# Differential attention on one Trainium2 core: steps of two query tiles in place of one

## What is computed

```
def attend_block(q_blk):
    s = jnp.einsum('mbhqd,mbhkd->mbhqk', q_blk, k).astype(jnp.float32) * scale
    p = jax.nn.softmax(s, axis=-1)
    a = p[0] - lam * p[1]
    return jnp.einsum('bhqk,bhkv->bhqv', a.astype(v.dtype), v)
...
o = rmsnorm(o, sub_gain) * (1.0 - lambda_init)
return o @ w_o
```

## Time and profile before

| | us |
|---|---|
| device time, median of 3 runs | 983.8 |
| lowest, highest | 982.41, 983.94 |
| span of the profiled execution, first to last instruction | 980.4 |
| attention in it, from the first scores to the MLP's first product | 77.8 to 281.3 |
| busy in the span: TensorE | 967.6 |
| VectorE | 853.5 |
| ScalarE | 457.9 |
| GpSimd | 377.8 |

### The profile page before, as it was taken

How to read it: one execution, slowest core, us unless ns; L and a number is a source line. 1 busy time by engine, 2 the same in 40 slices (tenths; PEclk the granted TensorE clock), 3 DMA queues, 4 the chain that set the end, 5 groups by cost and what they waited for, 6 DMA issues and landing times.

```text
span 980.4 us, 12869 instructions
## 1 busy us (share of the span) xinstructions
PE 967.6 (99%) x4684; PEld 796.9 (81%) x4684; DVE 853.5 (87%) x1157; ACT 457.9 (47%) x703; POOL 377.8 (39%) x333
## 2 busy tenths in 40 slices
PE   9999999989999999999999999999999999999998
PEld 7887877767887878888888888988888888888887
DVE  6696999999777999999989888779898988989883
ACT  6445654666556253552534534475345253452520
POOL 6841453335463828467534000551340413405000
PEclk9999999999999999999999999999999999999999
DMA  7333220200251432423334250304342332422202
GB/s 264 87 107 102 72 65 1 65 22 22 66 171 44 135 123 87 129 87 101 114 87 128 65 172 23 129 1 129 87 129 87 108 107 87 129 86 86 87 1 86
DMA packets 50966, 90.12 MB, mean 92 GB/s; under 512 B 8268, under 2 KB 9560, under 8 KB 50904
## 3 DMA queue, kind: packets, MB, share of 16 engines
q1 hardware_dynamic: 45456, 89.14, 29.0%
q10 hardware_dynamic: 5448, 0.17, 0.3%
HBM read 87.20 MB, written 2.10 MB: 91 GB/s over the span
## 4 chain that ended last, share of the span: by engine, by line
PE 63%; DVE 5%; POOL 2%; issue 1%; ACT 1%; POOLq 0%; DVEq 0%; ACTq 0%
PE bank L1711 32%; PE pair L1711 30%; POOL s_nsum L766 1%; DVE s_acc L1476 1%; DVE s_lbB_lo L1225 1%; DVE s_lt_lo L1225 1%; DVE s_w_lo L1198 1%; DVE s_acc L1545 0%; DVE s_s_raw L1461 0%; PE bank L2070 0%; DVE s_u_raw L1443 0%; PE pair L2058 0%; DVE s_hT_lo L1425 0%; POOL s_lt L792 0%; ACT s_hT_hi L1037 0%
## 5 line engine op out<-in xcount | busy, mean ns | idle before, releaser
L792 POOL TENSOR_TENSOR s_lt<-s_lbB,s_lbB 128x1024 f32<-128x1024 f32 x14 | 34.5, 2466 | 263.4 <-PE pair L1711 163.9
L1198 DVE TENSOR_TENSOR s_w_lo<-s_raw,s_w_hi 128x1024 fp32r<-128x1024 f32 x72 | 127.5, 1791 | 3.7 <-ACT s_w_hi L871 3.7
L1225 DVE TENSOR_TENSOR s_lbB_lo<-s_lbB,s_b_hi 128x1024 fp32r<-128x1024 f32 x64 | 119.0, 1883 | 0.0
L893 ACT ACTIVATE s_b_hi<-s_lbB 128x1024 fp32r<-128x1024 f32 x64 | 67.2, 1053 | 77.0 <-POOL s_lbB L792 32.9
L1711 PE MATMUL bank<-s_hT_hi,s_w_hi 128*128 128x512 f32 x256 | 100.2, 392 | 0.0
L1711 PE MATMUL pair<-s_hT_hi,s_w_hi 128*128 128x512 f32 x256 | 100.1, 391 | 0.0
L1711 PE MATMUL bank<-s_hT_hi,s_w_lo 128*128 128x512 f32 x256 | 99.6, 389 | 0.0
L1711 PE MATMUL bank<-s_hT_lo,s_w_hi 128*128 128x512 f32 x256 | 99.6, 389 | 0.0
L1711 PE MATMUL pair<-s_hT_hi,s_w_lo 128*128 128x512 f32 x256 | 99.6, 389 | 0.0
L1711 PE MATMUL pair<-s_hT_lo,s_w_hi 128*128 128x512 f32 x256 | 99.6, 389 | 0.0
L1057 ACT ACTIVATE s_u_raw<-s_u_raw 128x512 f32<-128x512 f32 x64 | 40.4, 632 | 111.6 <-DVE s_u_raw L1443 111.6
(11 more groups left out here) (268 smaller groups left out, 2699.3 us busy)
## 6 DMA issues: line engine op xcount, KB each, us to landing
s_raw<-in_mlp_w SPq DMA_DIRECT2D x64, 512.0 KB, 3.7
s_lbB<-in_mlp_w SPq DMA_DIRECT2D x64, 512.0 KB, 3.3
s_raw<-in_attn_w_qkv SPq DMA_DIRECT2D x24, 512.0 KB, 4.1
s_raw<-in_attn_w_o SPq DMA_DIRECT2D x8, 512.0 KB, 3.3
s_x_nat<-in_x SPq DMA_DIRECT2D x4, 512.0 KB, 6.4
out<-s_acc SPq DMA_DIRECT2D x7, 256.0 KB, 2.0
s_raw<-in_pool_w SPq DMA_DIRECT2D x4, 256.0 KB, 2.7
out<-s_acc SPq DMA_DIRECT2D x2, 128.0 KB, 1.8
```

The source lines that it names most:

```text
L792: g.tensor_tensor(w2_raw[n][:], w2_raw[one][:], w2_raw[two][:], ALU.subtract).then_inc(t_done, 1)
L893: a.activation(b_hi[home][:], w2_raw[n][:], ACT.Copy).then_inc(w2_hi_done, 1)
L1198: v.tensor_tensor(w_lo[slot][:, cols], raw[k][:], f32(w_hi[slot][:, cols]), ALU.subtract)\
L1225: v.tensor_tensor(w2_lo[n][:], w2_raw[n][:], f32(b_hi[home][:]), ALU.subtract).then_inc(w2_lo_done, 1)
```

## The change

A step `j` now handles a pair of query tiles, 2j and 2j+1, in 16 steps and a tail. The scores have four banks (both `pair` tensors, one per tile), the exponentials three buffers. The maxima of both maps of a tile are one reduction of 1024. Reciprocal and factor are computed once for a pair. The turned maps go to banks 4 and 5, which the sides use as well (q and k bank 4, o and the new turn back bank 5). `values(p)` takes V as weights and the turned maps of both tiles as moving operand, three matmuls of 256 columns per block of keys, so that o arrives transposed in bank 6. ScalarE copies it once per head (`keep_values`), TensorE turns it back (`turn_back`), ScalarE copies that (`keep_back`), and the statistics, the scaling and the turn of o follow as before. `o_keep` is gone. All fillers but the first use bank 7. The tables and the order in every engine's loop are written anew. The diff, cut to its core: lines of before that are replaced are left out where they stand in the listing above.

```
...
+    (((9, 0), (0, 1)), ((9, 1), (2,))),
+    (((10, 0), (0, 1)), ((10, 1), (2,))),
+    (((11, 0), (0, 1)), ((11, 1), (2, 3))),
+    (((12, 0), (0, 1)), ((12, 1), (2, 3))),
+    (((13, 0), (0, 1, 2)), ((13, 1), (3, 4))),
+    (((14, 0), (0, 1, 2)), ((14, 1), (3, 4))),
+    (((15, 0), (0, 1, 2)), ((15, 1), (3, 4, 5))),
+    (((16, 0), (0, 1, 2)), ((16, 1), (3, 4, 5))))
+X_SUMMED = (8, 8, 9, 10, 11, 12, 13, 14)
+X_ADDED = (11, 12, 13, 14, 15, 16, 18, 18)
+def filler_places():
+    at = {(u // 2, u % 2): divmod(max(u - 1, 0), 3) for u in range(2 * F_V)}
+    at |= {(f, u): (f - F_V + 5, u) for f in range(F_V, F_Y) for u in range(2)}
+        at |= {(f, u): place for u, (place, _) in enumerate(W_O_PARTS[f - F_Y])}
+FILL = filler_places()
+FILLED = {f: max(place for (g, _), place in FILL.items() if g == f) for f in range(F_END)}
+FILL_BANK = {f: 7 if f else 6 for f in range(F_END)}
+SPLIT = {4: (0, 0, 1, 1), 5: (2, 2, 3, 3), 6: (5, 5, 6, 6), 7: (10, 12, 13, 14), 8: (17, 17, 18, 18)}
...
+QK_SIDE = {j: (what, n) for j, what, n in SIDE if j >= 0 and what != "o"}
+O_SIDE = {j: (what, n) for j, what, n in SIDE if what == "o"}
...
         def turn_bank(what, n):
-            return bank[2 + n % 2] if what == "map" else bank[4]
+            if what == "map":
+                return bank[4 + n % 2]
+            return bank[5] if what == "o" else bank[4]
         def turn_scale(what):
...
+            def exps(n):
+                if n >= 3:
+                    act.wait_ge(turned, n - 2)
+                act.wait_ge(max_done, n + 1)
...
+                    a.activation(probs[n % 3][:, m, :], pair[n % 2][:, m, :], ACT.Exp,
+                                 bias=nmax[:, n % 4, m:m + 1],
+                                 accum_out=lsum[:, n, m:m + 1]).then_inc(exp_done, 1)
...
+            def keep_values(h):
+                act.wait_ge(pv_done, 2 * h + 2)
+                if h:
+                    act.wait_ge(back_turned, h)
+                a.activation(ov[:], bank[6][:], ACT.Copy).then_inc(ov_kept, 1)
+            def keep_back(h):
+                act.wait_ge(back_turned, h + 1)
+                if h:
+                    act.wait_ge(side_turned, SIDE_NO["o", h - 1] + 1)
+                a.activation(oc[:], bank[5][:], ACT.Copy).then_inc(back_kept, 1)
+            for j in range(END):
+                for f in range(F_END):
+                    if FILLED[f] == (j - 1, 2) or F_V <= f < F_Y and FILLED[f] == (j - 1, 1):
+                        filled(f)
+                if j < PAIRS:
+                    exps(2 * j)
+                for f in range(F_END):
+                    if FILLED[f] == (j, 0):
+                        filled(f)
+                if 1 <= j <= PAIRS:
+                    keep_turn("map", 2 * j - 2)
+                    keep_turn("map", 2 * j - 1)
+                if j < PAIRS:
+                    exps(2 * j + 1)
+                for f in range(F_END):
+                    if FILLED[f] == (j, 1) and not F_V <= f < F_Y:
+                        filled(f)
+                if j in QK_SIDE:
+                    keep_turn(*QK_SIDE[j])
+                if j in BACK:
+                    keep_back(BACK[j])
+                if j in KEPT:
+                    keep_values(KEPT[j])
+                if j in O_SIDE:
+                    keep_turn(*O_SIDE[j])
...
+            def maxima(n):
+                dve.wait_ge(scored, n + 1)
+                v.tensor_reduce(nmax[:, n % 4, :], pair[n % 2][:], AX.X, ALU.max, negate=True).then_inc(max_done, 1)
+            def mix_root(p):
+                dve.wait_ge(exp_done, 4 * p + 4)
+                v.reciprocal(rl1[:, p % 2, :], lsum[:, 2 * p:2 * p + 2, 1]).then_inc(mix_rooted, 1)
+            def mix_factor(p):
+                dve.wait_ge(mix_rooted, p + 1)
+                v.scalar_tensor_tensor(mixc[:, p % 2, :], lsum[:, 2 * p:2 * p + 2, 0], neg_lam[:, 0:1],
+                                       rl1[:, p % 2, :], ALU.mult, ALU.mult).then_inc(mix_known, 1)
+            def combine(n):
+                dve.wait_ge(mix_known, n // 2 + 1)
+                both = probs[n % 3]
+                v.scalar_tensor_tensor(both[:, 0, :], both[:, 1, :], mixc[:, n // 2 % 2, n % 2:n % 2 + 1], both[:, 0, :],
                                        ALU.mult, ALU.add).then_inc(a_done, 1)
+            def o_stats(h):
+                mine = lsum[:, NT * h:NT * h + NT, 0]
+                v.scalar_tensor_tensor(o_sq[:], mine, EPS, mine, ALU.mult, ALU.mult)
+                dve.wait_ge(o_squared, h + 1)
+                link(v.tensor_reduce(o_ss[:], osq[:].rearrange("p (t d) -> p t d", t=NT), AX.X, ALU.add))
+                if h:
+                    dve.wait_ge(o_normed, h)
+                v.scalar_tensor_tensor(o_v[:], o_ss[:], 1.0 / VD, o_sq[:], ALU.mult, ALU.add).then_inc(o_v_done, 1)
+            for j in range(END + 1):
                 for f in range(F_V, F_Y):
+                    if FILLED[f] == (j - 1, 1):
+                        v_lo_part(1, f - F_V, bank[FILL_BANK[f]])
+                if 1 <= j <= PAIRS:
+                    mix_root(j - 1)
+                    mix_factor(j - 1)
+                    combine(2 * j - 2)
+                    combine(2 * j - 1)
+                if j in STATS:
+                    o_stats(STATS[j])
+                if j < PAIRS:
+                    maxima(2 * j)
+                    maxima(2 * j + 1)
                 for f in range(F_V):
+                    if FILLED[f][0] == j - 1:
                         qk_sum(2 * NT + f)
+                if 1 <= j <= PAIRS:
+                    turn_lo("map", 2 * j - 2)
+                    turn_lo("map", 2 * j - 1)
                 for s, steps in SPLIT.items():
                     for k in range(4):
+                        if steps[k] + 1 == j:
                             split_lo(s, k, s % 2)
+                if j in QK_SIDE:
+                    turn_lo(*QK_SIDE[j])
+                for f in range(F_V):
+                    if FILLED[f][0] == j - 1:
+                        qk_norm(2 * NT + f)
+                if j in O_SIDE:
+                    turn_lo(*O_SIDE[j])
...
+                    step = n // 2
+                    if n % 2 == 0 and step in QK_SIDE:
+                        pe.wait_ge(side_lo_done, SIDE_NO[QK_SIDE[step]] + 1)
+                    elif n % 2 and step in O_SIDE:
+                        pe.wait_ge(side_lo_done, SIDE_NO[O_SIDE[step]] + 1)
+                    elif n % 2 and step in BACK:
+                        pe.wait_ge(back_kept, BACK[step] + 1)
+                    elif n >= 2:
+                        pe.wait_ge(turn_lo_done, n - 1)
...
                     else:
+                        pe.wait_ge(turn_lo_done, 4 * n - 5 + 2 * which)
...
+            def turn_back(h):
+                pe.wait_ge(ov_kept, h + 1)
+                if h < NH - 1:
+                    pe.wait_ge(turn_lo_done, 4 * h + 6)
+                else:
+                    pe.wait_ge(side_lo_done, SIDE_NO["o", h - 1] + 1)
+                for t in range(NT):
+                    last = nc.tensor.transpose(bank[5][:, t * P:(t + 1) * P], ov[:, t * P:(t + 1) * P], ident[:])
+                last.then_inc(back_turned, 1)
...
-                if i >= 1:
-                    pe.wait_ge(exp_done, 2 * i)
+                if n >= 2:
+                    pe.wait_ge(exp_done, 2 * n - 2)
+                else:
+                    pe.wait_ge(v_lo_done, 2 * n + 2)
...
+                        last = mm(pair[n % 2][:, m, :], lhs[rows, 0, cols], rhs[rows, 1, :], start=part == 0,
+                                  stop=part == 2)
...
+            def values(p):
+                h, late = divmod(p, 2)
+                pe.wait_ge(turn_lo_done, 2 * p + 2)
+                if p == 0:
+                    pe.wait_ge(qk_copied, 2 * NT + 1)
+                if not late:
+                    if h:
+                        pe.wait_ge(ov_kept, h)
+                dst = bank[6][:, late * 2 * P:(late + 1) * 2 * P]
+                    v_hi, v_lo = (val[half][:, part, k, cols] for part in range(2))
+                    last = three(dst, v_hi, v_lo, aT_hi[:, :, keys], aT_lo[:, :, keys], k == 0, k == NT - 1)
...
+                dst = bank[FILL_BANK[f]]
...
+            def fillers(j, slot):
+                for part, place in FILL.items():
+                    if place == (j, slot):
+                        filler(*part)
+            scores(0)
+            filler(0, 0)
+            scores(1)
+            filler(0, 1)
+            for j in range(PAIRS + 1):
+                if 1 <= j < PAIRS:
+                    scores(2 * j)
+                    scores(2 * j + 1)
+                if j == PAIRS:
+                    w_o_rest((0, 1), (3, 4, 5))
+                if j:
+                    fillers(j, 0)
+                    turn("map", 2 * j - 2)
+                    turn("map", 2 * j - 1)
+                fillers(j, 1)
+                if j in QK_SIDE:
+                    turn(*QK_SIDE[j])
+                if j in BACK:
```

(17 more changed lines are left out.)

279 lines of the change are left out of this document (78 added, 201 removed).

## The result

The kernel with the change takes 1007.33 us (median of 4 runs, 1006.18 to 1010.04), the kernel before on the same chip 983.11 (982.30 to 983.94). The ratio is 1.0254 with a 95% interval of 1.0242 to 1.0266: slower by 24.2 us. The direction was forecast, the time (988.0, range 972 to 998) was not. The profiled execution took 1008.38 us, with a span of 1006.6 us and a mean granted clock of 0.988.

A forecast was written before the change was run, and what follows sets the result against it. TensorE bounds attention now, VectorE second; afterwards a VectorE-ScalarE loop from step 6. Work -10.0, old waits -5.7, stalls +4, +15.4 and +0.5 make +4.2: span 980.4 to 984.6, plus 3.4 gives 988.0 us, range 972 to 998.

The forecast's parts named there:

- The new operations: On TensorE and VectorE: two score groups 1.67 us, values' matmuls 0.12 apart, a 1024-wide maximum 1.22 to 1.27.
- the chance kept for 0.17: Rival: 256-column matmuls on V stay at 0.17 us, adding 3 us; chance 0.04, together with anything unseen.
- The loop: VectorE and ScalarE wait on each other: 8.7 us per odd step, 10.7 per even; ruling from step 6, chance 0.48.
- the term for GpSimd: GpSimd delaying VectorE in the loop: 0.5 us per step, bounds 0.2 and 1.0.
- the clock: TensorE's granted clock in attention: 1.00 throughout, with gaps under 3 us found in no row with a lower one.
- Steps 0 to 4 ... No stall: TensorE's three filler halves cover the loop in steps 0 to 4: 13.1 us a step, stall bounds 0 and 1.
- 0.7 a step: Steps 6 to 8: V's next tile waits in the one filler bank for a copy and low part, 0.7 us more.
- The work: TensorE's net work in attention: scores -4.4, map turns -2.4, values -6.7, turning back +3.5, together -10.0 us.
- VectorE's list: VectorE's work in attention, with o_keep, double maxima and half the reciprocals and factors gone: net -20.1 us.
- So this adds nothing: Sides sharing banks 4 and 5 with the maps: low parts end before ScalarE is free, so 0 us added.
- forecast 70.4: Steps 9 to 15: four at 8.7, three at 10.7, plus 7 x 0.5, against TensorE's work of 55.0.
- (4): Rival: GpSimd holds VectorE 1.0 us or more per step, w_o splits stretch, steps 1 to 4 stall: 994 to 1003; chance 0.14.

The follow-up runs named there:

- experiment 3: Changed kernel with the square of o moved to ScalarE and GpSimd's residual sums held until both maxima of the step are done: 996.19 us.
- Experiments 2: Changed kernel with GpSimd's two residual sums done on only 8 of 512 columns: 1000.16 us.
- experiment 1: Changed kernel with 14 extra 256-column products issued by TensorE ahead of its long waits: 1003.83 us.
- experiment 4: Changed kernel with the maxima of a pair's first tile ahead of the previous pair's reciprocal, factor and combines on VectorE: 996.40 us.
- experiment 5: Changed kernel with first maxima ahead of the previous pair's mixing, square of o on ScalarE, GpSimd's sums behind the maxima: 991.92 us; both maxima first: 1007.54 us.

## Why the prediction was wrong in size

**The new operations were priced nearly right.** Two score groups in a row take 1.59 (91.70 to the filler behind them at 93.29 in the trace after) where the sum said 1.67, values run at a distance of 0.12, so the chance kept for 0.17 was not needed; a maximum of 1024 takes 1.22. What they replaced was not: see the fourth step below.

**The loop was right.** Steps 9, 11 and 13 take 8.6 where the sum said 8.7. Steps 10, 12 and 14 take 10.9 without GpSimd's overlap (experiment 3) where it said 10.7. Only step 15 is shorter, 7.4 for 8.7.

**The step that failed first is the term for GpSimd.** "I take 0.5, between them" was meant per step. Experiments 2 and 3 put it at nothing in the odd steps and 1.5, 2.5 and 2.5 in steps 10, 12 and 14: two combines longer by 1.0, 2.0 and 2.0, and the factor by 0.5. The lengths of these steps at full clock agree: 12.4, 13.4 and 13.4 with the overlap (experiment 1), 10.9 without (experiment 3). That is 6.5 us over the stretch instead of 3.5. It was priced as a mean over the old schedule, where the sums fell beside few combines; in the new tables the odd step's two sums stand behind the square in GpSimd's queue and are released with it, so those of an odd step fall on the next step's combines. The prediction had seen this for the square and not asked it of the sums, whose place stands in the diff (`X_ADDED`, `X_SUMMED`, behind `BACK` in GpSimd's queue). The Trainium skill ("SBUF — State Buffer", section "SBUF: two separate sides") lets a VectorE operation with two SBUF inputs and a GpSimd operation that reads SBUF exclude each other for the whole instruction. The runs agree: the combine of 0.74 beside sums took up to 1.78, and the maximum with its PSUM input (experiment 4) took its 1.22.

**The second is the clock.** The prediction took it to stay at 1.00, because gaps of the size expected stood in no row with a lower one. But such gaps stood in no row at all: the longest wait in attention was 1.1 us, so the trace said nothing about a gap of 2 to 3. With new gaps that long, the 1.00 should have been one end of a range. Experiment 1 puts the price at 6.2 us or more up to step 16.

**The third is "Steps 0 to 4 ... No stall".** Steps 1 to 3 took 12.8, 13.4 and 13.2 (scores at 91.70, 104.46, 117.87, 131.08), as forecast at 13.1. Step 4 took 18.0:

```profile
139.49 0.50 PE L1742 MATMUL bank<-s_w_hi,s_hT_hi 128*128 128x512 f32 x1 [2.94 <-ACT s_qs L934]
```

TensorE waited 2.94 us for ScalarE's copy out of bank 7 and lost 1.7 to the clock behind it (half of 3.41; with the gap filled, experiment 1, the step took 16.4). In experiment 5 the same step took 14.0. The change leaves one bank for fillers, and the prediction asked this of V's tiles only. It put 0.7 a step on them; the waits in steps 6 and 7 were 2.73 and 2.50, with the clock.

**The work is the fourth.** TensorE's gain was to be 10.0. At full clock (experiment 1) it is 197.8 - 192.9 = 4.9. Distances from start to start, summed by kind over that run and the kernel before: values 31.7 to 24.9 (6.8, forecast 6.7); scores 28.9 to 25.7 (3.2 for 4.4, since a single group cost 0.90 in the kernel before and not 0.98); map turns 13.4 to 13.3 (0.1 for 2.4, since a single turn cost 0.42 in the kernel before and not 0.50); the other turns 8.4 to 12.9 (4.5 more for 3.5); fillers and what else there is make the rest. In steps that the loop rules this costs nothing, in steps 0 to 5 and in the tail it counts. VectorE's list was to shrink by 20.1, and its busy time fell by 10.1. It had been summed from record lengths, and these overlap: by groups, the records of attention before add up to 199.8 us in 180.0 busy, those after to 177.2 in 169.9. No term of the sum rests on it.

**Side turns.** "So this adds nothing" fell as well: with VectorE late by the overlap, TensorE waited 13.3 us there and at the values of step 14. In experiment 3, without the overlap and at full clock from step 9 on, it still waited 2.52, 1.80, 1.92, 1.11 and 1.24 us in front of the side turns of steps 9 to 13; in experiment 5 only one such wait is over 1 us (1.33). What sharing banks 4 and 5 costs by itself no run tells, since the values behind the side turn wait for the same low parts.

Put together for steps 9 to 15: forecast 70.4. Out go the 3.5 for GpSimd, 66.9 (65.9 in experiment 3). With 6.5 for the overlap 72.4 to 73.4 (72.4 in experiment 1, at full clock), and 75.3 with the half clock in the kernel itself. For the rest, the reciprocal of step 6 came 7.1 later than forecast (163.83 for 156.7), 4.9 of it from step 4, steps 6 to 8 took 37.8 for 32.9, and from the last reciprocal to the MLP 30.4 for 25.5 (what the forecast leaves up to 285.5; it has no sum of its own for the tail), where TensorE is idle for 2.0 (put at 0.5) and busy for the rest. The four differences, 7.1, 4.9, 4.9 and 4.9, are the 21.8 us by which the MLP starts later than 285.5.

**Of the rivals**, (4) named the right parts (GpSimd, a stall ahead of step 5) with too small a price, 994 to 1003. It left out the clock; at full clock the kernel took 1003.8 (experiment 1), just above its range. The direction came out right because the loop was right; the size did not, since all four steps above erred toward too fast. What remains argued and not shown: how the 2.2 us up to step 6 that aren't step 4's divide, what the tail's 4.9 consist of, what a second maximum ahead of the mixing costs by itself, and what VectorE's and ScalarE's even step of 9.9 would need to get shorter.

## What to carry to other kernels

A price for two engines in each other's way belongs to the overlap, not to the operation: when the order changes, look which operations the new releases put side by side, and price those, not the old mean. When a change is expected to open gaps that the old trace doesn't have, that trace says nothing of the clock behind them, and half clock is the other end of the range. And where a bank is single, its readers belong in their queues where the next writer needs them, not where the next step begins: here that was worth 3.6 us with the overlap gone (1.7 with it still there), while moving the writer cost 5.5.
